# Threshold search of a two-layer mixer kernel: counts spread over TensorE's work, elementwise products moved to GpSimd

## The chip, the cores and the metric

The kernel runs on one core of a Trainium2 chip. The metric is the time on the device in microseconds (us), the lower the better. Three runs of the kernel before gave 668.64, 673.66 and 677.35 us; their median is 673.66 us.

## The reference, cut to what matters

Two layers of a mixer are computed for one prompt of 256 tokens and for 8 sequences with 4 new tokens each, so 288 token columns in all, and in each layer three branches: sparse attention whose keys are chosen by an indexer (the 256 best of 2,052 positions for a sample token), dilated window attention, and a state-space scan (SSD). Everything is float32.

```python
for l in range(DEPTH):                                    # 2 layers
    hp, kv, ki, dil, conv, ssd = layer_prompt(hp, prm)
    hs, kv, ki, dil, conv, ssd = layer_sample(hs, cache_dsa_kv, cache_dsa_kidx, l, page_table, dil_bufs, ...)

# in a layer
(q_a, k_a, v_a, g_a, qi, ki, wi, q_c, k_c, v_c, g_c, z, xbc, dt) = project(rms_norm(x, norm_w), w_in)
q_a, k_a, qi, ki, q_c, k_c = rope_partial(...)            # x * cos + partner(x) * sin
sc = indexer_scores(qi, wi, ki_all)
_, idx = lax.top_k(sc, n_sel)                             # found here as a threshold
o_a = sparse_attend(q_a, k[idx], v[idx])
o_c, new_bufs = dilated_sample(q_c, k_c, v_c, bufs)       # new_bufs: the old cache, shifted by 4
seg = acs[i] - acs[j];  scores = (C B^T) * exp(seg) * dt  # SSD, 6 heads
y = y_diag + (C h_in) * exp(acs);  y = (y + d_skip * xs) * silu(z)
x = x + merge_out(o_a, g_a, o_c, g_c, y, w_out)
```

The outputs include the shifted window caches (`new_bufs`), which are copies from memory to memory.

## The kernel before, in words

**Tiling.** A layer projects the 288 columns through 35 weight tiles of 128 output rows (QI 0 to 3, KI 4, QA 5 and 6, XBC 7 to 13, KA 14 and 15, ZZ 16 to 18, QC 19 to 21, KC 22 to 24, VC 25 to 27, GC 28 to 30, VA 31 and 32, GA 33 and 34), each 8 steps of k (`proj(i)`), and through 8 tiles of the output matrix. The code is written by hand, one program for each engine, with semaphores between them; the order of each program is the order of the work, and no scheduler changes it. All matrix products go through one helper, `mm` (L825), all transposes through `turn` (L875).

**Weights.** A tile's weights are 512 KB. Four slots hold them; SyncE's queue (SP) loads tile i + 4 when tile i has been computed (`next_w`, L425).

**Cache records.** The pages of keys and values and the windows go through a ring of 8 slots. A slot is loaded again when TensorE has used it, in turn by SP and by GpSimd's queue (L404, L397).

**Cache copies.** `keep(b, use)` (L496) issues three copies from memory to memory on GpSimd's queue, 2,044, 508 and 124 KB for a sequence, once projection tile `use` has been computed: tiles 16 to 21, 23 and 24.

**The search.** The 256th best score is found bit by bit. In `compare(n)` (L1453) VectorE compares 516 scores in each of 128 rows with the trial value and sums the hits; in `bit_count(n)` TensorE adds up the row segments in one small product; in `settle(n)` (L1464, L1466) VectorE sets the bit. That is done 32 times, and each step needs the one before. Between them stand, on TensorE, the projection tiles 16 to 26 with three counts in each tile (after k steps 2, 5 and 7), the transposes of the SSD inputs, and the six SSD heads (`head(h)`), which end with the row of decays for the head after the next (`bc`). On VectorE stand, after a compare and ahead of its settle, the rotary products (`rope`, L1408 to L1413: a shuffle and three products of 128x288), the inputs of the state sums (`state_inputs`, L1716), the heads' exponents and factors (`lin`, `g_mul`) and the gated outputs (`y_out`, L1755 and L1759). GpSimd has `masked` (L518: the state inputs of one sequence) and the spreading of the dilated queries (L539, L543).

**After it.** With the threshold known, a mask is built (L1943), spread by TensorE, added to the scores (L1949), and the exponentials (L766) are transposed; then come the value records, the other projections and the output product.

Of the kernel before, what the change touches and what calls it, by code (L numbers as in the profile page):

```python
# [18 lines left out]
ALU = mybir.AluOpType  # L19
# [3 lines left out]
P = 128  # L23
# [3 lines left out]
TP = 256  # L27
# [107 lines left out]
def bank_plan():  # L135
# [33 lines left out]
    for name, bank in (("ad", 7), ("xs0", 5), ("bt0", 3), ("bt1", 2), ("xs2", 6), ("xs1", 7), ("bt2", 3), ("knt", 6), ("cb", 2),  # L169
                       ("lastj", 6), ("cbs", 6), ("st0", 5), ("st1", 3)):  # L170
        use(name, bank)
# [25 lines left out]
    "rstd_ready": 1, "sq_ready": 8, "sq_used": 7, "y_normed": 8, "xw_ready": 8, "xn_free": 7, "xn_ready": 8, "roped": 15, "ssum_ready": 1, "root_ready": 1,  # L197
# [4 lines left out]
    "dec_ready": 1, "xws_ready": 1, "ea_ready": 6, "lin": 6, "lexp": 6, "g_ready": 6, "yh_used": 3, "dn_used": 1,  # L202
# [7 lines left out]
def build(nc, a):  # L210

    plan, _ = bank_plan()
    with ExitStack() as ctx:
        def sb(name, shape, dt=F32):
# [16 lines left out]
        tmp = sb("tmp", [P, T])  # L231
        misc = sb("misc", [64, T])
# [76 lines left out]
             for name in ("x_in0", "x_in1", "ptab_in", "prm_in", "cst_in", "const_in", "ones_set", "zeroed", "act_chain", "dve_chain", "y_out",  # L309
# [69 lines left out]
        def w_count(layer, i):  # L379

            return 16 * ((layer * NW + i) // WSLOTS + 1)

# [100 lines left out]
        def _(pool):  # L483
            POOL = mybir.EngineType.Pool
            pool.wait_ge(S["ptab_in"], 16)
# [3 lines left out]
            for L in range(DEPTH):  # L489
# [30 lines left out]

                keep(0, "proj16")
# [3 lines left out]
                keep(1, "proj17")  # L525
                keep(2, "proj18")
                pool.wait_ge(S["xws_ready"], nth(L, "xws_ready", 1))
# [12 lines left out]
                for g in range(3):  # L540
                    for h2 in range(2):
                        q = ptile(QC + g, TP, T, half(h2)).rearrange("p (b q) -> p b q", q=NQ)
                        pool.tensor_copy(qcbd[half(h2), g, :, h2:2 * NB:2], q.rearrange("p b q -> p q b")).then_inc(S["qcbd_ready"], 1)  # L543
                keep(6, "proj23")
                keep(7, "proj24")
                consumed(*RING[32:40])
# [25 lines left out]
        def _(act):  # L572
# [20 lines left out]
            for L in range(DEPTH):  # L593
# [137 lines left out]
                evac(18)  # L731
                act.wait_ge(S["adt_ready"], nth(L, "adt_ready", 1))
                act.activation(dec[:, 0:2, :], dec[:, 0:2, :], ACT.Exp).then_inc(chain.next(), 1)
                act.activation(dec[0:32, 2, :], dec[0:32, 2, :], ACT.Exp).then_inc(S["dec_ready"], 1)
                evac(19)
                act.wait_ge(filled("cbs"), nth(L, "cbs"))
                act.activation(cbs[:, :], bank_of("cbs")[0:32, 0:64], ACT.Copy).then_inc(drained("cbs"), 1)
                act.wait_ge(filled("st0"), nth(L, "st0"))
# [3 lines left out]
                evac(20)  # L742

                def ssd_exp(h):
# [3 lines left out]
                    if h >= 2:  # L748
                        act.wait_ge(S["g_ready"], nth(L, "g_ready", h - 1))

                    act.wait_ge(S["lin"], nth(L, "lin", h + 1))
                    act.activation(ea[:, h % 2, :], src[:, 0:T], ACT.Exp).then_inc(S["ea_ready"], 1)
# [3 lines left out]
                    act.activation(lg[0:32, h % 2, TP:T], lg[0:32, h % 2, TP:T], ACT.Exp, bias=nacs[0:32, 2, h:h + 1]).then_inc(S["lexp"], 1)  # L756

# [63 lines left out]
        def _(pe):  # L821
# [16 lines left out]
            for L in range(DEPTH):  # L838
# [13 lines left out]
                def proj(i, *counts):  # L852


                    at = {len(counts): (3, 7)[:len(counts)], 3: (2, 5, 7)}[len(counts)]

                    wt = weights(i)
                    pe.wait_ge(drained(f"proj{i}"), before(L, f"proj{i}"))
                    out = bank_of(f"proj{i}")
                    for k in range(KT):  # L860
# [4 lines left out]
                        ins = mm(out[:, 0:T], wt[:, k, :], xn[:, k, :], start=(k == 0), stop=(k == KT - 1))  # L865
                        if i == LATE_ROOT - 1 and k < KT - 1:
                            ins.then_inc(S["xn_free"], 1)
                        if k in at and k < KT - 1:
                            bit_count(counts[at.index(k)])
                    ins.then_inc(filled(f"proj{i}"), 1)  # L870
                    if KT - 1 in at:
                        bit_count(counts[-1])
# [242 lines left out]
                proj(16, 0, 1, 2)  # L1115
# [6 lines left out]
                ins.then_inc(filled("ad"), 1)  # L1122
                pe.wait_ge(S["conved"], nth(L, "conved", 7))
# [5 lines left out]
                proj(17, 3, 4, 5)  # L1129
                token_rows("xs", 1, XBC, 3)  # L1130
                token_rows("bt", 2, XBC + 3, 2)
                pe.wait_ge(S["roped"], nth(L, "roped", 9))
# [6 lines left out]
                pe.wait_ge(drained("cb"), before(L, "cb"))  # L1139
                out = bank_of("cb")  # L1140
                for g in range(2):
                    for c in range(2):
                        ins = mm(out[:, g * 256 + c * P:g * 256 + (c + 1) * P], ptile(XBC + 3 + g, c * P, (c + 1) * P),
                                 ptile(XBC + 5 + g, c * P, (c + 1) * P))
                ins.then_inc(filled("cb"), 1)

                proj(18, 6, 7, 8)
                pe.wait_ge(drained("ad"), nth(L, "ad"))
# [1043 lines left out]
```

## Time and profile before

| | us |
|---|---|
| median of 3 runs | 673.66 (668.64 to 677.35) |
| the profiled execution, its own time | 673.8 |
| its span, first to last instruction | 672.1 |
| TensorE busy (matmul) | 611.9 (91%) |
| VectorE, GpSimd, ScalarE busy | 377.8, 224.0, 168.1 |
| chain that ended last: TensorE, VectorE, DMA | 63%, 15%, 13% |
| mean granted TensorE clock | 0.962 |
| moved by DMA | 198.38 MB, 295 GB/s in the mean |

The search of the first layer lies at 113 to 202 us of the span, that of the second at 435 to 525 us. A granted clock of 1.0 is 2.4 GHz, 0.5 is 1.2 GHz. An instruction that waits shows its wait as idle time ahead of it, with what ended it.

### The profile page before, as it was taken

Reading aid. Unit: us, or ns where it says so; the run is one execution under the profiler, and the core shown is the slowest. Engines: PE = TensorE matmul, PEld = TensorE weight load, DVE = VectorE, ACT = ScalarE, POOL = GpSimd, SP = SyncE. Lnnn points to the kernel's source line nnn. Section 1 sums busy time; section 2 is a strip of 40 time slices with the busy share of each in tenths; the row PEclk is TensorE's granted clock in tenths of the full one; section 3 lists DMA queues with packets and bytes.
Section 4 is the critical chain, followed back from the end, with each engine's and each line's share of the span. In section 5 each row is a group of like instructions: output and inputs, shape, how many; then the busy total and the mean of one; then the engine's idle time right before and its main releaser. Section 6 shows DMA issues by size and latency. Waiting matters only on the chain.

```text
span 672.1 us, 13786 instructions
## 1 busy us (share of the span) xinstructions
PE 611.9 (91%) x4870; PEld 426.9 (64%) x4870; DVE 377.8 (56%) x1150; ACT 168.1 (25%) x405; POOL 224.0 (33%) x406
## 2 busy tenths in 40 slices
PE   5999998888899989999999999988888989789994
PEld 3766564665567665667776656566665867556772
DVE  3765565677569545443167475577756855343413
ACT  3024222121113312451101433212201151126211
POOL 0507530241206676451000664124120377642000
PEclk9999999898889998999999999999878999889998
DMA  7979999999968989996334999999997598996031
GB/s 294 308 274 356 368 369 413 417 358 331 353 236 262 314 305 369 366 329 234 110 121 134 323 368 369 402 413 355 349 394 265 181 333 287 374 357 214 10 118 70
DMA packets 67766, 198.38 MB, mean 295 GB/s; under 512 B 11537, under 2 KB 40370, under 8 KB 66418
## 3 DMA queue, kind: packets, MB, share of 16 engines
q1 hardware_dynamic: 49682, 99.99, 42.8%
q0 software_dynamic: 18016, 97.50, 40.3%
q8 instruction: 39, 0.64, 0.4%
q14 instruction: 29, 0.24, 0.1%
HBM read 189.30 MB, written 52.00 MB: 359 GB/s over the span
## 4 chain that ended last, share of the span: by engine, by line
PE 63%; DVE 15%; DMA 13%; ACT 4%; issue 2%; SPq 2%; DVEq 0%; ACTq 0%
PE bank L825 60%; DMA w<-in_w 5%; DMA kv<-in_vv 4%; DMA kv<-in_kk 4%; DVE hit L1453 3%; PE bank L875 3%; SPq L404 2%; DVE tb L1466 1%; DVE st L1955 1%; ACT srow L766 1%; ACT shared L663 1%; DVE tb L1464 1%; DMA x<-in_x 1%; DVE shared L1576 1%; ACT shared L680 1%
## 5 line engine op out<-in xcount | busy, mean ns | idle before, releaser
L825 PE MATMUL bank<-xn,w 128*128 128x288 f32 x1120 | 307.0, 429 | 0.7 <-DMA w<-in_w 0.7
L825 PEld LDWEIGHTS bank<-xn,w 128*128 128x128 f32 x1120 | 213.9, 198 | 74.9 <-issue 19.1
L404 POOL DMA_DIRECT2D kv<-in_vv x160 | 86.3, 539 | 96.9 <-PE bank L825 69.5
L404 POOL DMA_DIRECT2D kv<-in_kk x128 | 68.8, 538 | 144.5 <-issue 96.1
L616 ACT ACTIVATE pt<-bank 128x288 f32<-128x288 f32 x48 | 19.6, 409 | 243.4 <-PE bank L825 243.4
L825 PE MATMUL bank<-pt,w 128*128 128x288 f32 x256 | 64.9, 407 | 0.0
L825 PEld LDWEIGHTS bank<-pt,w 128*128 128x128 f32 x256 | 48.3, 190 | 13.6 <-issue 0.8
L496 POOL DMA_DIRECT2D out_keep<-in_buf x48 | 23.5, 495 | 85.1 <-PE bank L825 78.7
L1453 DVE TENSOR_SCALAR_CACHE_REDUCE hit<-sc,tb 128x516 bf16<-128x516 f32 x62 | 46.5, 750 | 2.2
L825 PE MATMUL bank<-kv,pt 128*32 128x256 f32 x512 | 37.5, 404 | 11.0 <-DMA kv<-in_vv 10.7
L1464 DVE TENSOR_SCALAR tb<-bank 128x1 int32<-128x1 f32 x62 | 9.5, 153 | 48.7 <-PE bank L825 48.5
L825 PE MATMUL bank<-kv,qz 128*32 128x256 f32 x512 | 34.3, 385 | 0.0
L2022 DVE TENSOR_TENSOR x<-x,bank 128x288 f32<-128x288 f32 x16 | 7.3, 455 | 43.6 <-PE bank L825 43.3
L825 PEld LDWEIGHTS bank<-cnt,seg 128*128 128x128 f16 x68 | 6.9, 103 | 38.8 <-issue 36.7
L825 PE MATMUL bank<-cnt,seg 128*128 128x1 f16 x68 | 11.2, 169 | 21.8 <-DVE hit L1453 21.1
L1426 DVE COPY tails<-cin 128x3 f32<-128x3 f32 x14 | 7.2, 512 | 41.0 <-ACT cin L614 38.9
L825 PEld LDWEIGHTS bank<-kv,pt 128*32 128x32 f32 x512 | 14.1, 112 | 22.5 <-DMA kv<-in_vv 9.5
L825 PE MATMUL bank<-kv,shared 128*32 128x128 f32 x768 | 26.8, 285 | 0.0
L825 PE MATMUL bank<-pt 64*128 64x128 f32 (+3 forms) x168 | 26.3, 334 | 0.0
L518 POOL TENSOR_SCALAR xwb<-xws,const 32x384 f32<-32x384 f32 x16 | 21.2, 1329 | 13.4 <-DVE xws L1716 7.7
L583 ACT ACTIVATE phased<-x 128x288 f32<-128x288 f32 x24 | 10.5, 442 | 60.0 <-DVE x L2022 57.1
L825 PEld LDWEIGHTS bank<-pt 64*128 64x128 f32 (+2 forms) x168 | 17.9, 183 | 10.6 <-issue 9.8
(238 smaller groups left out, 796.7 us busy)
## 6 DMA issues: line engine op xcount, KB each, us to landing
w<-in_w SPq DMA_DIRECT2D x86, 512.0 KB, 7.3
out_keep<-in_buf POOLq DMA_DIRECT2D x16, 2044.0 KB, 13.0
kv<-in_kk SPq DMA_DIRECT2D x128, 160.0 KB, 8.2
kv<-in_kk POOLq DMA_DIRECT2D x128, 160.0 KB, 5.8
kv<-in_vv POOLq DMA_DIRECT2D x160, 128.0 KB, 5.6
kv<-in_dil SPq DMA_DIRECT2D x24, 576.0 KB, 7.5
kv<-in_vv SPq DMA_DIRECT2D x96, 128.0 KB, 7.3
out_keep<-in_buf POOLq DMA_DIRECT2D x16, 508.0 KB, 8.5
```

Source lines behind the costliest of these rows:

```text
L404: engine.dma_start(kv[:, s, r * rec:(r + 1) * rec], a["kk" if what == "page" else "vv"][bass.ds(page + layer * N_POOL, 1)].rearrange("o p ...
L496: pool.dma_start(a[f"keep{g}"][ly, b], a[f"buf{g}"][ly, b, 4 * 256:]).then_inc(S["copied"], 16)
L518: pool.tensor_scalar(xwb[:, b % 2, :], xws[0:32, 2, :], C("bm", b, b + 1, slice(0, 32)), None, ALU.mult).then_inc(S["xwb_ready"], 1)
L583: act.activation(squares[:, k % 2, 0:T], x[:, k, :], ACT.Square).then_inc(S["sq_ready"], 1)
L616: act.activation(ptile(i), src[:, 0:T], fn).then_inc(use, 1)
L663: act.activation(psa[:, i, 0:nk], psa[:, i, 0:nk], ACT.Exp, bias=st8[:, 1, i:i + 1], accum_out=st8[:, 2, i:i + 1]).then_inc(S["pexp"] if i ...
L825: return pe.matmul(out, lhsT, rhs, start=start, stop=stop, skip_group_check=True, **k)
L875: return pe.transpose(out, in_, ident(n))
L1426: dve.tensor_copy(tails[:, n, 0:3], cin[:, n % 2, TP:TP + 3]).then_inc(chain.next(), 1)
L1453: ts_(hit[:, :], sc[:, :], old.bitcast(F32), 0.0, ALU.is_ge, ALU.add, accum_out=cnt[:, 0:1]).then_inc(S["cnt_ready"], 1)
L1464: ts_(tb[:, 2:3], src[:, 0:1], float(TOPK_S), float(bit), ALU.is_lt, ALU.mult).then_inc(drained(f"count{n}"), 1)
L2022: tt_(x[:, m, :], x[:, m, :], src[:, 0:T], ALU.add).then_inc(drained(f"out{m}"), 1)
```

## The change

Counts may now stand at any k step of a tile: `proj(i, lo, hi)` computes a part of a tile, and the counts are written between parts of tiles, groups of transposes and halves of heads. Five kinds of work go from VectorE to other engines. The three products of seven ropes (n = 8 to 14), the state inputs and the gating of y go to GpSimd; the shuffle stays on VectorE and gets a second buffer, `rstd`. The two small copies to `ebc` go to ScalarE. Three memsets that only signalled are gone. The cache copies keep their conditions, but GpSimd's program has other work ahead of and between them. The mask products move from between window products 5 and 6 into tile 27, after its second k step; tile 20 now comes before the `knt` products and the state sums, and `cb` and `lastj` before tile 18.

```diff
@@ GpSimd
+                def rope(n):
+                    i, s = ROPED[n], partner[n % 2][:, :]
+                    pool.wait_ge(S["shuffled"], nth(L, "shuffled", n - 7))
+                    pool.tensor_tensor(s, s, C("sin"), ALU.mult).then_inc(chain.next(), 1)
+                    pool.tensor_tensor(ptile(i), ptile(i), C("cos"), ALU.mult).then_inc(chain.next(), 1)
+                    pool.wait_ge(S["pool_chain"], chain.n)
+                    pool.tensor_tensor(ptile(i), ptile(i), s, ALU.add).then_inc(S["roped"], 1)
...
+                rope(8)
                 keep(0, "proj16")
...
                 keep(1, "proj17")
+                state_inputs()
                 keep(2, "proj18")
...
                 keep(3, "proj19")
+                rope(9)
                 keep(4, "proj20")
+                rope(10)
                 keep(5, "proj21")
+                rope(11)
...
+                rope(12)
                 keep(6, "proj23")
+                y_gated(0)
+                rope(13)
                 keep(7, "proj24")
+                rope(14)
+                y_gated(1)
+                y_gated(2)
                 consumed(*RING[32:40])
@@ TensorE
-                proj(16, 0, 1, 2)
+                proj(16, 0, 5)
+                bit_count(0)
+                proj(16, 5)
...
+                for h in range(1, 5):
+                    if h < 4:
+                        bit_count(13 + 3 * h)
+                    else:
+                        bit_count(25)
+                    proj(21 + h, 0, 5)
+                    bit_count(14 + 3 * h)
+                    proj(21 + h, 5)
+                    head(h, 15 + 3 * h)
+                proj(26, 0, 2)
+                bit_count(28)
+                proj(26, 2, 6)
+                bit_count(29)
+                proj(26, 6)
+                head(5, 30)
                 window_keys(0)
-                window_keys(1)
+                bit_count(31)
@@ VectorE
                 compare(17)
-                rope(10)
+                lin(2)
                 settle(17)
-
                 compare(18)
+                shuffle(12)
                 settle(18)
...
-                y_out(2)
...
-                rope(14)
```

TensorE's program, first at tile 22 and head 1 (`xn,w` are k steps of the tile, `cnt,seg` is a count, `cacc,xw`, `cs,xws` and `cs,phased` are the head, `ad,const` is `bc`). Before:

```order
L825 MATMUL bank<-xn,w 128x288 x3
L825 MATMUL bank<-cnt,seg 128x1
L825 MATMUL bank<-xn,w 128x288 x3
L825 MATMUL bank<-cnt,seg 128x1
L825 MATMUL bank<-xn,w 128x288 x2
L825 MATMUL bank<-cnt,seg 128x1
L825 MATMUL bank<-cacc,xw 64x128 x2
L825 MATMUL bank<-cacc,xw 64x32
L825 MATMUL bank<-cs,xws 64x128
L825 MATMUL bank<-cs,phased 64x4 x8
L825 MATMUL bank<-ad,const 128x288
```

The same place now:

```order
L872 MATMUL bank<-xn,w 128x288 x5
L872 MATMUL bank<-cnt,seg 128x1
L872 MATMUL bank<-xn,w 128x288 x3
L872 MATMUL bank<-cacc,xw 64x128 x2
L872 MATMUL bank<-cacc,xw 64x32
L872 MATMUL bank<-cs,xws 64x128
L872 MATMUL bank<-cnt,seg 128x1
L872 MATMUL bank<-cs,phased 64x4 x8
L872 MATMUL bank<-ad,const 128x288
L872 MATMUL bank<-cnt,seg 128x1
```

There are three counts for a tile and a head in both, but the gaps between them, in k steps, were 3, 2 and 3 with a head inside the last; now they are 5, 3 with the first part of the head, and the head's second part with `bc`.

VectorE's program around compare 20 (`hit` is the compare, the two `tb` rows are the settle). Before:

```order
L1453 TENSOR_SCALAR hit,cnt<-sc,tb 128x516
L1408 STREAM_SHUFFLE tmp<-pt 128x288
L1410 TENSOR_TENSOR tmp<-tmp,const 128x288
L1411 TENSOR_TENSOR pt<-pt,const 128x288
L1413 TENSOR_TENSOR pt<-pt,tmp 128x288
L1464 TENSOR_SCALAR tb<-bank 128x1
L1466 TENSOR_SCALAR tb<-tb 128x1
```

And now, around compares 21 and 22:

```order
L1550 TENSOR_SCALAR hit,cnt<-sc,tb 128x516
L1517 STREAM_SHUFFLE rstd<-pt 128x288
L1561 TENSOR_SCALAR tb<-bank 128x1
L1563 TENSOR_SCALAR tb<-tb 128x1
L1550 TENSOR_SCALAR hit,cnt<-sc,tb 128x516
L1827 TENSOR_TENSOR cs<-ea,pt 128x160
L1829 TENSOR_TENSOR cacc<-cacc,bank 128x256
L1830 TENSOR_TENSOR cacc<-cacc,cbs 32x32
```

Of a rope only the shuffle is left between a compare and its settle, and a head's factors no longer share a slot with the next head's exponents.

GpSimd's program from the copies behind tile 21 on. Before:

```order
L496 DMA out_keep<-in_buf 16x1984
L496 DMA out_keep<-in_buf 16x8128
L496 DMA out_keep<-in_buf 32x16352
L539 COPY shared<-pt 64x32 x6
L543 COPY qcbd<-pt 64x4x8 x6
```

And now:

```order
L502 DMA out_keep<-in_buf 16x1984
L502 DMA out_keep<-in_buf 16x8128
L502 DMA out_keep<-in_buf 32x16352
L531 TENSOR_TENSOR rstd<-rstd,const 128x288
L532 TENSOR_TENSOR pt<-pt,const 128x288
L534 TENSOR_TENSOR pt<-pt,rstd 128x288
L575 COPY shared<-pt 64x32 x6
L579 COPY qcbd<-pt 64x4x8 x6
L531 TENSOR_TENSOR tmp<-tmp,const 128x288
L532 TENSOR_TENSOR pt<-pt,const 128x288
L534 TENSOR_TENSOR pt<-pt,tmp 128x288
```

Two ropes now stand between these copies and those behind tile 23, each of which waits for a shuffle.

## Rows read from the trace of the kernel before

**Rows 1.** The page: DMA throughput in 40 equal slices of the span.

```profile
GB/s 294 308 274 356 368 369 413 417 358 331 353 236 262 314 305 369 366 329 234 110 121 134 323 368 369 402 413 355 349 394 265 181 333 287 374 357 214 10 118 70
```

**Rows 2.** Waits of TensorE: waiter, releaser, us in total, times, longest.

```profile
PE bank L825 <- DVE hit L1453: 21.1, 20, 1.7
PE bank L825 <- DMA kv<-in_vv: 10.7, 8, 2.6
PE bank L825 <- DMA w<-in_w: 0.7, 1, 0.7
```

**Rows 3.** Timeline of TensorE, tile 22 to 23 of layer 2: start, us, work.

```profile
474.96 0.16 PE L825 MATMUL bank<-cnt,seg 128*128 128x1 f16 x1 [1.20 <-DVE hit L1453]
475.19 0.85 PE L825 MATMUL bank<-cacc,xw 128*64 128x128 f32 x6
...
476.24 1.04 PE L825 MATMUL bank<-cs,phased 128*64 128x4 f32 x16
477.21 0.81 PE L825 MATMUL bank<-ad,const 6*128 6x288 f32 x2
477.95 3.25 PE L825 MATMUL bank<-xn,w 128*128 128x288 f32 x6
...
485.14 0.16 PE L825 MATMUL bank<-cnt,seg 128*128 128x1 f16 x1 [1.23 <-DVE hit L1453]
...
532.62 4.15 PE L825 MATMUL bank<-xn,w 128*128 128x288 f32 x16
```

**Rows 4.** Windows, the heads' stage of each layer: busy, clock, DMA share, GB/s.

```profile
155.00:203.00 48.00, 42.92 (x240) 30.55 (x239) 31.18 (x121) 6.35 (x21) 5.90 (x18) 0.86 0.84 304
480.00:527.00 47.00, 41.07 (x237) 28.89 (x239) 30.10 (x115) 6.75 (x23) 5.89 (x18) 0.84 0.85 304
```

**Rows 5.** Timeline of VectorE, a search step with nothing else in it.

```profile
146.47 0.75 DVE L1453 TENSOR_SCALAR_CACHE_REDUCE hit<-sc,tb 128x516 bf16<-128x516 f32 x1
...
147.58 0.16 DVE L1464 TENSOR_SCALAR tb<-bank 128x1 int32<-128x1 f32 x1 [0.35 <-PE bank L825]
...
148.02 0.75 DVE L1453 TENSOR_SCALAR_CACHE_REDUCE hit<-sc,tb 128x516 bf16<-128x516 f32 x1
```

**Rows 6.** Groups by line, VectorE at 112 to 209 us: a rope product.

```profile
L1410 DVE TENSOR_TENSOR tmp<-tmp,const 128x288 f32<-128x288 f32 x7 | 3.2, 458 | 0.2
```

**Rows 7.** DMA queues at 140 to 170 us: packets, MB, share.

```profile
q0 software_dynamic: 383, 9.45, 88.4%
q1 hardware_dynamic: 358, 1.30, 13.6%
```

**Rows 8.** The chain that ended last, at 460 to 500 us.

```profile
467.85 30.89 DMA w<-in_w
```

**Rows 9.** Loads of weights at 160 to 170 us, and of all 11 at 112 to 205 us.

```profile
w<-in_w SPq DMA_DIRECT2D x1, 512.0 KB, 23.5
...
DMA to landing us min/median/max: 3.4/14.5/25.6
```

**Rows 10.** Timeline of TensorE: tile 22's end, the window products of each layer, the transposes.

```profile
161.94 1.22 PE L825 MATMUL bank<-xn,w 128*128 128x288 f32 x4
...
203.29 1.52 PE L825 MATMUL bank<-kv,shared 128*32 128x128 f32 x48
...
216.33 1.09 PE L875 MATMUL bank<-const,srow 128*128 128x128 f32 x8 [0.70 <-ACT srow L766]
...
526.50 1.52 PE L825 MATMUL bank<-kv,shared 128*32 128x128 f32 x48
```

**Rows 11.** Groups by line, GpSimd, both layers.

```profile
L518 POOL TENSOR_SCALAR xwb<-xws,const 32x384 f32<-32x384 f32 x16 | 21.2, 1329 | 13.4 <-DVE xws L1716 7.7
L543 POOL COPY qcbd<-pt 64x32 f32<-64x32 f32 x12 | 3.2, 263 | 0.7
```

**Rows 12.** The chain that ended last, first layer, around the mask.

```profile
209.56 1.88 DVE srow L1949 x3
...
214.18 2.10 ACT srow L766 x2
```

More of the change, by code:

```diff
@@ L850, in weights, with proj @@
                     return w[:, slot, :, :]
[L852 to L860, printed above, removed]
+                def proj(i, lo=0, hi=KT):
+                    wt = w[:, (L * NW + i) % WSLOTS, :, :]
+                    if lo == 0:
+                        weights(i)
+                        pe.wait_ge(drained(f"proj{i}"), before(L, f"proj{i}"))
+                    for k in range(lo, hi):
                         if i == 0:
@@ L1127, in _ @@
                 token_rows("xs", 2, XBC, 3)
-                proj(17, 3, 4, 5)
+                proj(17, 0, 1)
+                bit_count(2)
+                proj(17, 1, 6)
+                bit_count(3)
+                proj(17, 6)
                 token_rows("xs", 1, XBC, 3)
                 token_rows("bt", 2, XBC + 3, 2)
+                bit_count(4)
+                pe.wait_ge(drained("cb"), before(L, "cb"))
+                out = bank_of("cb")
+                for g in range(2):
+                    for c in range(2):
+                        ins = mm(out[:, g * 256 + c * P:g * 256 + (c + 1) * P], ptile(XBC + 3 + g, c * P, (c + 1) * P),
+                                 ptile(XBC + 5 + g, c * P, (c + 1) * P))
+                ins.then_inc(filled("cb"), 1)
+                pe.wait_ge(drained("ad"), nth(L, "ad"))
+                pe.wait_ge(drained("lastj"), before(L, "lastj"))
+                out = bank_of("lastj")
+                for c in range(2):
+                    mm(out[:, 6 * c:6 * c + 6], C("lastp"), adt[:, c, 0:6])
+                mm(out[0:32, 12:18], C("last", rows=slice(0, 32)), adt[0:32, 2, 0:6]).then_inc(filled("lastj"), 1)
+                bit_count(5)
+                proj(18, 0, 4)
+                bit_count(6)
+                proj(18, 4)
+                bit_count(7)
+                proj(19, 0, 4)
+                bit_count(8)
+                proj(19, 4)
+                bit_count(9)
+                pe.wait_ge(drained("cbs"), before(L, "cbs"))
+                out = bank_of("cbs")
+                for g in range(2):
+                    ins = mm(out[0:32, g * 32:g * 32 + 32], ptile(XBC + 3 + g, TP, T), ptile(XBC + 5 + g, TP, T))
+                ins.then_inc(filled("cbs"), 1)
+                proj(20, 0, 3)
+                bit_count(10)
+                proj(20, 3, 7)
+                bit_count(11)
+                proj(20, 7)
                 pe.wait_ge(S["roped"], nth(L, "roped", 9))
```

210 lines of the change are left out of this document (104 added, 106 removed).

## The prediction

> **What bounds the kernel now.** I read four things in this order: what TensorE waits for, its timeline in the search, the granted clock there, and what the DMA queues carry meanwhile.
>
> TensorE is busy for 91% of the span, and in the table of its waits one line stands out: 21.1 us in 20 waits for the compare of the search; weights cost it 0.7 us, value records 10.7 us [rows 2]. The timeline of a tile and a head shows where [rows 3]. The third count comes two k steps after the second, 1.2 us of work [rows 10], but a bare search step takes 1.55 us from one compare to the next [rows 5], and before this count VectorE had more to do. So TensorE stands 1.2 us, does the head, whose second half is 16 tiny products, and `bc`, and then the first six matmuls of the next tile take 3.25 us, where a whole tile of 16 takes 4.15 us elsewhere [rows 3]. Six should take 1.55 us: 1.7 us are lost to the clock, which is 0.86 and 0.84 in the mean of the two heads' stages [rows 4] and so falls from 2.4 to 1.2 GHz in each of these stretches. The clock did not fall behind the last two heads of the first layer, where the stall was 1.06 us and no `bc` followed, or where it was 0.24 us. One period is 10.18 us (474.96 to 485.14) [rows 3].
>
> The third party is DMA. It is 84% busy in these stages [rows 4], and from 101 to 185 us it moves 331 to 417 GB/s [rows 1]. At 140 to 170 us the queue of the cache copies (q0) moves 9.45 MB and that of the weights (q1) 1.30 MB, with nearly the same number of packets, 383 and 358 [rows 7]. The engines take them in turn, and a copy's packet is seven times as large, so weights come in at 43 GB/s, 12 us for a tile of 512 KB, as long as copies are queued. A load then takes 23.5 us [rows 9], and once 30.9 us: the load of tile 24 of the second layer starts when tile 20 ends, at 467.85, and lands when tile 24 wants to start [rows 8]; that is the 0.7 us of wait [rows 2].
>
> **The change part by part.**
>
> *Counts between parts of tiles.* The 32 steps of a layer were 1.2 to 1.7 us apart where VectorE needs 1.55 us plus its extra work. I set the new gaps on TensorE against VectorE's need. A k step is 0.5 us, so the gaps in the heads' stage are 5 k steps (2.6 us), 3 k steps and the head's first part (1.55 + 1.05), and the second part with `bc` (1.0 + 0.75). VectorE's longest extra work there is a head's factors (about 0.9 us, of which 0.35 us hide in the count's own latency [rows 5]), 2.1 us in all. Only two early gaps (ahead of counts 2 and 13) come out short, by 0.1 and 0.3 us. So the stall of 10.6 us per layer goes, 21.1 us in all, less about 1 us.
>
> *The clock.* With no stall ahead of a head the 1.7 us behind it should go too: four times in the first layer, five in the second, 15.3 us, and 1.7 us once early in the first layer.
>
> *Work moved from VectorE.* Seven ropes lose three products of 0.46 us each per layer [rows 6], y gating three, the state inputs three. All lay beside TensorE's work or are in the stalls counted above, so I add nothing. The copies to `ebc` on ScalarE: nothing, it is 25% busy and a head has 7 us.
>
> *GpSimd.* It takes 21 rope products, 3 state products and 3 gating products per layer. None is in the trace. From below, a product costs VectorE's 0.46 us [rows 6]; from above, twice the 1.33 us that GpSimd takes for a one-input product of 384 columns [rows 11], cut to 288, is 2.0 us. I take 1.3 us, nearer the row of the same engine, so a rope is 4 us. Every tile period gives it one rope, 1.5 us of issuing copies, and once 3.6 us of spreading: it keeps up. Copies leave up to 2 us late, which costs nothing while the copies before them are still queued. The Trainium skill (GPSIMD Engine Reference, "Performance versus the Vector engine") measures a two-input product of 2,048 columns at 4,497 ns against 2,293 ns; by that one of 288 columns would be near 0.9 us, an estimate, and the sum would be the same.
>
> *GpSimd beside VectorE.* In the 3.6 us in which GpSimd spreads queries, VectorE's product takes 0.46 us as ever, so I take 0. If VectorE's work were stretched by a fifth, the gaps above would still cover it.
>
> *The mask.* VectorE goes from mask to scores without `rope(14)`, but TensorE now has only 6 k steps of tile 27 (3.1 us) and 2.3 us of small products between the mask product and the transposes, while additions, maximum and exponential take 6.7 us (209.56 to 216.28) [rows 12] and start 0.25 us after. TensorE waits some 1.4 us where it waited 0.7 [rows 10]: +0.7 us per layer.
>
> *The weights.* All of this moves TensorE's wish for tiles 20 to 26 forward, and the copies' too, but not the bytes. By the parts above, a period in the heads' stage is a tile of 4.1 us, a head of 2.0 and a `bc` of 0.75: 6.9 us instead of 10.2. The weights' queue, however, is never empty: loads are asked for every 5 to 10 us, when a tile ends, and land 14.5 us later in the median [rows 9]. So an earlier request lands no earlier. In the first layer the load of tile 26 starts when tile 22 ends (161.94 + 1.22) and lands 23.5 us later [rows 9, 10], at 186.8 us; tile 26 and the last head take 6.1 us, so the window products start at 192.9 us where they started at 203.3 [rows 10]: a gain of 10.4 us. In the second layer tile 24 cannot start before 498.8 [rows 8]; it and its head take 6.9 us, tile 25 6.2 (no `bc`), tile 26 6.1: 518.0 instead of 526.5 [rows 10], a gain of 8.5 us. The tiles between land within these bounds. Without the weights the same points would come at 182 and 504 us.
>
> **The sum.** 10.4 + 8.5 = 18.9 us, less 1.4 us for the two masks, less 1.7 us for one slow stretch behind the long wait that tile 24 of the second layer then has (8 us): 15.8 us. The profiled execution took 673.8 us, 0.1 us from the median of three, so 658 us. The Trainium skill (DMA: Bandwidth & Descriptors, "Queues, rings and completion order") says that each DMA engine goes round its queues by packets, and the equal packet counts agree with it; it speaks for the weights keeping their small share. If they had half of the bytes instead, a load would land in 3 to 4 us and the sum would be the second rival's.
>
> **The rivals.**
>
> *Same pace* (chance 0.22). Weights land up to 2 or 3 us later than I assume, since the copies are asked for earlier too; each wait at a tile's start stands beside a weak head, so the slow clock stays for several tiles, and the last of them is not hidden. For it: the weights' rate of 12 us a tile is above the old period of 10.2 us, and loads in the second layer are later than in the first. Then 2 to 10 us are gained: 664 to 672, say 667.
>
> *Weights keep up* (chance 0.17). A deeper queue or copies that leave later let loads land with the requests. Stalls and clock give 21.4 and 22.1 us, less 1.4: 632 us. But the copies still need their time: 10 us of their traffic in each layer would then run into the value records, for which TensorE waits already [rows 2]. With that 640 to 650, say 645.
>
> *GpSimd sets the pace* (chance 0.06, the slower side). Its program is one queue: products, then copies, then the loads of value records. From the copies of tile 19 to the first value load it has 70 us now, less 11 us of copies and spreading, for 21 products: 2.8 us each. Above that value loads and window queries come later than before; at 3.5 us it is 15 us per layer, 700 us with the gain gone. Against it: both bounds above lie below 2.8 us. It decides only from there.
>
> *The clock stays low* though stalls go, because the heads' tiny products are enough: that is inside the first rival and my own range, since waiting for weights hides it.
>
> My forecast has 0.55. Its own range is 650 to 665.
>
> **The numbers.** 658 us; the range of 642 to 671 leaves out the best part of the second rival, the third, and the end of the first. The runs before spread by 9 us, so 2% (13.5 us) is about what can be told from no change. Faster by over 2% means under 660.2: six tenths of my forecast and all of the second rival with a part of the first, 0.54. Within 2%: 0.39. Slower: 0.07.
>
> **What would show it.** The waits for compares under 3 us instead of 21.1. New waits of TensorE for `in_w`, 10 to 25 us in all, at the starts of tiles 22 to 26, with loads that take over 25 us. The packets of the two queues near one to one while copies run. GpSimd's product of 288 columns at 0.7 to 2.0 us, and its value loads no later after the last head than before. Granted clock in the heads' stage over 0.86. Window products 10 and 8 us earlier against the start of the search. I am wrong if TensorE waits neither for weights nor for compares (then it is the second rival), or if the wait for weights is there and the ends do not move (the first).

## The result and the profile after

The change makes the kernel slower by 1.8%: 685.55 us (682.46 to 689.48, 4 runs) against 674.07 us (668.64 to 677.35, 4 runs), a ratio of 1.018 with a 95% interval of 1.013 to 1.024. It is slower beyond the noise, but whether by more than 2% is not settled. The forecast was 658 us with a range of 642 to 671. The profiled execution took 684.6 us; its span is 682.9 us, 10.8 us over that of the kernel before. In all that follows a median is that of all runs of a kernel, and a ratio leaves out runs that took over 1.5% more than the quickest.

TensorE's waits in the changed kernel (columns as in [rows 2]):

```profile
PE bank L872 <- DMA w<-in_w: 17.6, 7, 3.6
PE bank L872 <- DMA kv<-in_vv: 8.1, 7, 2.6
PE bank L917 <- ACT srow L813: 4.4, 2, 2.2
PE bank L872 <- DMA kv<-in_kk: 3.6, 5, 1.4
PE bank L872 <- ACT xws L787: 2.0, 2, 1.0
```

The wait for the compare, 21.1 us in [rows 2], is gone from the table. Waits for weights have taken its place, 17.6 us where there were 0.7. Two waits for ScalarE are larger or new: for the exponentials (2.2 us in each layer) and for the copies of the state sums (1.0 us).

TensorE's timeline in the first layer shows where (start, us, work, the wait ahead in brackets):

```profile
169.37 4.38 PE L872 MATMUL bank<-xn,w 128*128 128x288 f32 x10 [1.20 <-DMA w<-in_w]
181.98 5.17 PE L872 MATMUL bank<-xn,w 128*128 128x288 f32 x10 [3.57 <-DMA w<-in_w]
194.60 2.29 PE L872 MATMUL bank<-xn,w 128*128 128x288 f32 x4 [3.58 <-DMA w<-in_w]
204.19 0.86 PE L872 MATMUL bank<-kv,shared 128*32 128x128 f32 x24
204.99 0.18 PE L872 MATMUL bank<-cnt,seg 128*128 128x1 f16 x1
...
219.05 3.83 PE L917 MATMUL bank<-const,srow 128*128 128x128 f32 x16 [2.21 <-ACT srow L813]
```

Tiles 24, 25 and 26 each wait for weights, and ten matmuls behind such a wait take 4.4 to 5.2 us, where ten take 2.7 us elsewhere (a row of e1 below). The window products start at 204.19; they started at 203.29 [rows 10]. The transposes, which started at 216.33 [rows 10], start 2.7 us later, and the 16 of them take 3.83 us.

The chain that ended last, around the end of each search, now runs through the load of tile 26:

```profile
157.91 36.64 DMA w<-in_w
...
486.92 39.06 DMA w<-in_w
```

The load lands at 194.55 in the first layer, 36.64 us after it was asked for; [rows 8] had 30.89 us at the worst. The queues at 140 to 170 us:

```profile
q0 software_dynamic: 384, 9.49, 89.5%
q1 hardware_dynamic: 381, 1.36, 13.6%
...
w<-in_w SPq DMA_DIRECT2D x3, 512.0 KB, 31.8
```

As many packets on one queue as on the other, those of the copies seven times as large in the mean, 45 GB/s for the weights: the picture of [rows 7], with a median landing time of 31.8 us. (What these counts hold is looked at under e10.) The heads' stages, as in [rows 4]:

```profile
155.00:203.00 48.00, 39.65 (x199) 27.34 (x197) 25.31 (x83) 7.16 (x29) 14.30 (x29) 0.82 0.86 300
480.00:527.00 47.00, 37.72 (x205) 26.69 (x204) 24.66 (x85) 8.08 (x35) 18.15 (x35) 0.83 0.98 342
```

The granted clock (the third number from the end) did not rise from 0.86 and 0.84; it fell to 0.82 and 0.83.

**Where the 10.8 us lie.** Four points of TensorE's timeline cut the span: the first window product of each layer (the search has ended), and the single transpose ahead of the output product. I use the same cuts for the experiments.

| kernel (span) | search 1 ends | to output 1 | to end of search 2 | to output 2 | rest |
|---|---|---|---|---|---|
| before (672.1) | 203.3 | 102.9 | 220.3 | 106.0 | 39.6 |
| after (682.9) | 204.2 | 110.4 | 220.9 | 107.8 | 39.7 |
| e1 after, no copies (648.1) | 188.6 | 109.0 | 202.3 | 108.6 | 39.6 |
| e2 before, no copies (671.0) | 204.5 | 106.2 | 215.5 | 105.2 | 39.6 |
| e5 two copies behind the search (674.4) | 192.0 | 116.4 | 208.1 | 118.1 | 39.7 |
| e8 tile 28 earlier (672.4) | 203.3 | 105.3 | 218.6 | 105.6 | 39.7 |
| e10 copies in smaller rows (694.5) | 188.7 | 133.0 | 204.3 | 128.8 | 39.7 |
| e13 copies asked for later (670.0) | 198.1 | 109.7 | 210.6 | 111.9 | 39.6 |
| e15 best (650.5) | 187.9 | 102.6 | 208.3 | 106.5 | 45.2 |

So the searches gained nothing (+0.9 and +0.6 us), and 9.3 us were lost between the searches and the output products. A row is one execution: that of e8 is the quickest of its six (674.1 us, where the median is 679.6), that of e13 the slowest of its four (671.7, where the median is 667.2).

The experiments ran in groups, each beside the kernel before, whose median was 671.6 to 676.2 us. Ratios are to that of the same group; a difference in us between kernels of two groups can be off by some 5 us.

### The profile page after: what moved, and what is told of

Its sections match the earlier page's. It is cut to its first block, busy times and chain, and to the rows that moved or that the text cites. A ratio compares the mean times of both kernels' runs of the same rounds, so it can differ in the third digit from the quotient of the medians.

```text
span 682.9 us, 13776 instructions
## 1 busy us (share of the span) xinstructions
PE 623.0 (91%) x4870; PEld 435.0 (64%) x4870; DVE 359.0 (53%) x1058; ACT 175.8 (26%) x433; POOL 267.1 (39%) x460
## 4 chain that ended last, share of the span: by engine, by line
PE 64%; DMA 21%; DVE 6%; ACT 4%; SPq 2%; issue 2%; ACTq 0%; DVEq 0%; POOLq 0%; POOL 0%
PE bank L872 61%; DMA w<-in_w 11%; DMA kv<-in_kk 6%; DMA kv<-in_vv 3%; PE bank L917 3%; SPq L409 2%; DVE shared L1673 1%; DVE st L2032 1%; ACT srow L813 1%; ACT shared L707 1%; DVE xw L1860 1%; ACT shared L724 1%; DVE st L1679 1%; DVE srow L2026 1%; DMA x<-in_x 1%
## 5 line engine op out<-in xcount | busy, mean ns | idle before, releaser
L872 PE MATMUL bank<-xn,w 128*128 128x288 f32 x1120 | 311.2, 435 | 17.6 <-DMA w<-in_w 17.6
L872 PEld LDWEIGHTS bank<-xn,w 128*128 128x128 f32 x1120 | 218.5, 201 | 93.4 <-DMA w<-in_w 18.2
L872 PE MATMUL bank<-kv,pt 128*32 128x256 f32 x512 | 39.6, 422 | 10.7 <-DMA kv<-in_vv 8.1
L872 PEld LDWEIGHTS bank<-kv,shared 128*32 128x32 f32 x768 | 22.9, 118 | 4.3 <-issue 2.3
L872 PEld LDWEIGHTS bank<-pt 64*128 64x128 f32 (+2 forms) x168 | 17.9, 183 | 11.0 <-issue 10.2
L550 POOL TENSOR_TENSOR pt<-pt 128x288 f32<-128x288 f32 x6 | 4.8, 798 | 48.8 <-DVE pt L1836 48.8
```

The source lines that it names most:

```text
L872: return pe.matmul(out, lhsT, rhs, start=start, stop=stop, skip_group_check=True, **k)
```

## The experiments

**Theory.** Weights and copies share the DMA engines by packets. At the new pace tiles ask for weights every 7.3 us, and the copies, which wait for tiles, are asked for earlier as well. They go ahead of the weights of the last tiles, so the search ends when it ended before. Rivals: GpSimd's new work costs the time; the new order itself is worse; what is taken from one stage only reappears in the next.

**e1 and e2, without the copies.** What does the order give when nothing competes with the weights?

```diff
-                    for g in range(3):
-                        pool.dma_start(a[f"keep{g}"][ly, b], a[f"buf{g}"][ly, b, 4 * 256:]).then_inc(S["copied"], 16)
...
-            pool.wait_ge(S["copied"], DEPTH * PER["copied"])
```

> The changed kernel with the window cache copies left out (its output lacks them). Packet turns (the copies' large packets starve the weights' queue): TensorE's waits for weights in the heads' stage fall from 17.6 us in all to under 2, the clock there rises above 0.95, the window products of the first layer start 18 to 22 us earlier than 204.2, and the kernel takes 630 to 645 us. GpSimd or the new order itself is what costs: the search ends where it did, within 5 us of 204.2, and the kernel stays above 665 us.

> The kernel before with the window cache copies left out (its output lacks them). It is the partner of the kernel above. Packet turns: its search waits for compares, not for weights, so the 21 us of stalls and the slow clock stay and only the waits for value records shrink: 660 to 670 us, so the new order is worth 20 to 30 us without copies. If the new order is what costs, this one is the faster of the two.

Measured: 651.51 us (ratio to before 0.971, 0.964 to 0.978) and 672.12 us (0.998, 0.995 to 1.002). The changed order alone is worth 20.6 us. The copies cost the kernel before nothing and cost the changed one 34 us, 15.6 and 18.6 us of it in the two searches (the table). Both runs are 2 to 7 us above what was expected, and the window products of e1 start 15.6 us earlier, not 18 to 22. Waits of TensorE in e1:

```profile
PE bank L869 <- DMA kv<-in_vv: 11.8, 9, 3.7
```

No line for weights is left in its table. The expected 630 to 645 us was too low by 6: one reason is in its timeline, at the start of tile 23 of the first layer:

```profile
157.66 1.09 PE L869 MATMUL bank<-cs,phased 128*64 128x4 f32 x16
158.68 0.75 PE L869 MATMUL bank<-ad,const 6*128 6x288 f32 x2
159.36 0.18 PE L869 MATMUL bank<-cnt,seg 128*128 128x1 f16 x1
159.40 4.31 PE L869 MATMUL bank<-xn,w 128*128 128x288 f32 x10
...
168.28 2.67 PE L869 MATMUL bank<-xn,w 128*128 128x288 f32 x10
```

TensorE stands nowhere here, and still the ten matmuls at 159.40 run at half clock; those at 168.28 do not.

**e3 and e4, copies in rows of 4 KB**, written in alternating order so that rows are not joined again.

```diff
-                        pool.dma_start(a[f"keep{g}"][ly, b], a[f"buf{g}"][ly, b, 4 * 256:]).then_inc(S["copied"], 16)
+                        n = (992, 1016, 1022)[g]
+                        dst, src_ = (v.rearrange("o (r two n) -> (o two) r n", two=2, n=n)
+                                     for v in (a[f"keep{g}"][ly, b], a[f"buf{g}"][ly, b, 4 * 256:]))
+                        pool.dma_start(dst, src_).then_inc(S["copied"], 16)
```

> The changed kernel with the same copies in rows of 4 KB in alternating order, so that a packet of a copy is no larger than one of the weights. Packet turns: the weights' queue gets near half of the bytes, the waits for weights in the search fall from 17.6 us to under 4, window products of the first layer start 12 to 20 us earlier, the copies end later and run into the value records; 645 to 660 us. Total bandwidth is the bound: loads of weights land no earlier, or the whole traffic is slower with small packets, and the kernel takes 680 us or more.

> The kernel before with the copies in rows of 4 KB. Packet turns: it waits 0.7 us for weights, so it has nothing to win and the copies may reach further into the value records: 668 to 680 us. Total bandwidth, with small packets less efficient: above 680 us, and the same loss would lie in the changed kernel.

Measured: 934.09 and 933.24 us, ratio 1.391 for both. A load of weights in the search of e3 landed in 8.3 us in the median, against 22.8 in the changed kernel. The times fall under the second expectation of each, 680 us and more, but in form only: I did not expect a loss of 260 us. In the trace the copies' packets have 8,176 bytes, the size of two rows, so they are still twice the 4 KB of the weights'. And something larger happened. GpSimd's timeline in e3:

```profile
131.12 1.43 POOL L505 DMA_DIRECT2D out_keep<-in_buf  x2
173.38 1.60 POOL L505 DMA_DIRECT2D out_keep<-in_buf  x1 [40.82 <-issue]
```

Between two parts of one copy GpSimd stands 40.8 us with nothing that it waits for; I read it as a full queue, which no row names. Everything behind it in its program comes late, ropes and value loads. So this pair says little about shares.

**e10, rows of 16 KB**, the milder form of the same question: `n = (992, 4064, 4088)[g]`.

> The changed kernel with copies in rows of 16 KB for the two large parts, same places, same bytes. Shares go by packets: the weights' queue gets a larger share of the bytes beside copies, a load in the search lands in under 25 us where it took 31.8, waits for weights fall below 10 us while the copies end later, 676 to 684 us. Shares do not depend on the size of packets: landing times and waits as before, 684 to 688 us. GpSimd held up in issuing, as with rows of 4 KB: waits for compares come back, above 700 us.

Measured: 697.11 us (1.035, 1.030 to 1.041). The time is outside all three expectations, but the parts are the clearest of the study. The queues at 150 to 190 us in e10:

```profile
q0 software_dynamic: 3456, 11.23, 74.1%
q1 hardware_dynamic: 712, 2.61, 17.5%
```

The same stretch of the changed kernel:

```profile
q0 software_dynamic: 477, 12.18, 87.0%
q1 hardware_dynamic: 477, 1.76, 13.3%
```

Beside shorter rows the weights get 2.61 instead of 1.76 MB of nearly the same total. A load in the search lands in 12.5 us in the median instead of 22.8, TensorE waits for no weights at all, and the first search ends at 188.68 us, as without copies (188.55). The copies pay: they land in 33.2 us instead of 18.2 and reach far into the next stage, where TensorE then waits for value records:

```profile
PE bank L875 <- DMA kv<-in_vv: 46.8, 13, 15.4
```

The weights were starved by their share, and that share depends on the length of the copies' rows. How the engines take turns these runs do not settle. By the rows above the packets stand 4.9 to 1 in e10 and one to one in the changed kernel, but many of them carry next to nothing. All packets of e10 in that stretch, and those of the changed kernel:

```profile
DMA packets 4170, 13.87 MB, mean 347 GB/s; under 512 B 2821, under 2 KB 2821, under 8 KB 3499
...
DMA packets 956, 13.97 MB, mean 349 GB/s; under 512 B 249, under 2 KB 249, under 8 KB 743
```

Those under 512 bytes are of 4 and 8 bytes. Without them the copies' queue has 710 packets to 637 of the weights' in e10, nearly one to one, and 276 to 429 in the changed kernel, where they are of 64, 32 and 8 KB against 4 KB.

**e5, two copies behind the search.** The copies of sequences 6 and 7 leave behind tile 26.

```diff
-                keep(6, "proj23")
...
-                keep(7, "proj24")
...
                 feat(KC, KC + 3, 5)
+                keep(6, "proj26")
+                keep(7, "proj26")
                 masked(2)
```

> The changed kernel with the last two copies of each layer (sequences 6 and 7, asked for at tiles 23 and 24) moved behind tile 26 and the key columns' output. Demand above supply: while tiles take 7 us, eight copies and the weights want more than the engines move, and the weights are the side that waits; without two copies the waits for weights in the search fall from 17.6 to under 5 us and the first window products start 10 to 14 us earlier, but the two copies then run beside the value records: 664 to 678 us. New order or GpSimd at fault: 683 us or more.

Measured: 678.07 us (1.008, 1.004 to 1.011), at the upper edge of the expectation; the waits for weights are 6.4 us, not under 5. Waits:

```profile
PE bank L872 <- DMA kv<-in_vv: 17.2, 11, 3.6
...
PE bank L872 <- DMA w<-in_w: 6.4, 2, 3.4
```

The searches end 12.2 and 12.8 us sooner, the stages behind them take 6.0 and 10.4 us longer: two thirds of the gain is given back there. The waits for value records have grown by 9.1 us (17.2 against 8.1), which is a good half of the 16.4.

**e6, the same two copies in the output product**, `keep(6, "out0")` and `keep(7, "out4")` at the end of GpSimd's layer.

> The changed kernel with the same two copies of each layer moved to the output product (behind its tiles 0 and 4), where DMA is at half load. Demand above supply: the search as in the kernel above, the value records no later than without copies, the output tiles perhaps 2 to 5 us slower: 654 to 666 us. New order or GpSimd at fault: 683 us or more.

Measured: a median of 673.69 us in ten runs that spread from 661.4 to 677.7, the widest of all. It is above the expectation, but 12 us below the changed kernel.

**e7, the seven ropes back on VectorE.**

```diff
-                shuffle(12)
+                rope(12)
```

(the same for 8 to 11, 13 and 14, and the seven `rope` calls gone from GpSimd's program)

> The changed kernel with the three products of the seven ropes back on VectorE, everything else as changed. GpSimd's products are innocent (they take 0.8 us and copies never leave late): the time stays within 1% of 685 us, a little more if VectorE now makes TensorE wait. GpSimd's products are the cost, by delayed issues or by slowing VectorE: 670 to 677 us.

Measured: 684.99 us (1.016, 1.009 to 1.024), the changed kernel's 685.55. The rope products on GpSimd are innocent (its state inputs and gating stayed there). The waits of TensorE say more:

```profile
PE bank L865 <- DMA w<-in_w: 9.9, 4, 4.2
PE bank L865 <- DVE hit L1543: 7.6, 12, 0.7
```

7.6 us of waits for compares came back, and the waits for weights shrank from 17.6 to 9.9 us. Together they are 17.5 us, and the window products start at 204.29 us where they started at 204.19: whoever makes TensorE wait, the search ends when the weights have come.

**e8, tile 28 ahead of the transposes.** It fills the wait for the exponentials.

```diff
                 state_sum(1)
+                proj(28)
                 pe.wait_ge(S["sexp"], nth(L, "sexp", 1))
...
                 value_groups(0, 4)
-                proj(28)
```

> The changed kernel with projection tile 28 ahead of the transposes of the exponentials instead of behind the first value products. Late mask: the two waits of 2.2 us for the exponentials and the half clock behind them (16 transposes in 3.8 us) go, 679 to 682 us. The value records set the time of that stage: no gain, 684 to 687 us.

Measured: 679.59 us (1.010, 1.003 to 1.017). The transposes:

```profile
219.84 1.04 PE L917 MATMUL bank<-const,srow 128*128 128x128 f32 x8
221.19 1.14 PE L917 MATMUL bank<-const,srow 128*128 128x128 f32 x8 [0.31 <-ACT pt L820]
```

The wait of 2.21 us is gone and the half clock with it: the two halves take 1.04 and 1.14 us, the 16 took 3.83. From search to output it gains 5.1 and 2.2 us. For the whole kernel the gain is not clear of noise by this run alone (the intervals, 1.003 to 1.017 and 1.013 to 1.024, overlap); e9 and e14 below bear it out.

**e9, e11, e12, combinations.** e9 is e6 with e8; e11 moves three copies, behind output tiles 0, 3 and 6; e12 is e9 with the first decay rows two k steps later, to fill the wait of 1.0 us for ScalarE:

```diff
+                proj(21, 0, 2)
+                bit_count(13)
                 bc(0)
-                bit_count(13)
                 bc(1)
-                proj(21, 0, 3)
+                proj(21, 2, 5)
                 bit_count(14)
-                proj(21, 3)
+                proj(21, 5)
```

> The changed kernel with two copies of each layer in the output product and tile 28 ahead of the transposes, both edits of the two runs before together. The two losses are separate (the copies' bytes in the search, and the late mask): the gains add, 12 and 6 us, and it takes 665 to 670 us. They are one loss (value records arrive at the same time whatever comes before): 672 us or more.

> Three copies of each layer (sequences 5, 6 and 7) in the output product, behind its tiles 0, 3 and 6, and tile 28 ahead of the transposes. Demand above supply in the search: no wait for weights is left there (under 2 us), but three copies in 50 us of output product may cost 3 to 6 us there; 658 to 668 us. If a third copy only moves the wait to the output tiles: as with two copies, 665 to 672 us.

> As the kernel with two copies moved and tile 28 earlier, and the first two decay rows behind two k steps of tile 21, so that TensorE need not wait 1.0 us for ScalarE's copy of the state sums. Stall and half clock behind it (6 steps in 3.25 us, 10 in 4.17) go: 3 to 6 us less than the kernel without this edit. The weights set the search's end anyway: the same time within 1 us.

Measured: 665.15 us (0.988, 0.982 to 0.994), 672.46 us (0.999, 0.994 to 1.003) and 663.43 us (0.986, 0.980 to 0.992). e9 did as expected. e11 missed: with the third copy 12.9 us of waits for weights lie in the output products of both layers, the longest in the first, and 4.6 us are still in the searches, where under 2 were expected:

```profile
319.16 6.76 PE L872 MATMUL bank<-pt,w 128*128 128x288 f32 x16 [5.12 <-DMA w<-in_w]
```

In e12 the wait for ScalarE is gone, but it is only 1.7 us below e9 and within the spread of both, between its two expectations (3 to 6 us less, or the same within 1), which leaves that edit open.

**e13, the copies asked for about when they were before.** The step of the forecast that failed is tested: TensorE keeps the new order, only the copies wait for later tiles (18, 19, 20, 21, 22, 24 and 25 instead of 17 to 21, 23 and 24).

```diff
-                keep(1, "proj17")
                 state_inputs()
-                keep(2, "proj18")
+                keep(1, "proj18")
...
-                keep(3, "proj19")
+                keep(2, "proj19")
                 rope(9)
-                keep(4, "proj20")
+                keep(3, "proj20")
                 rope(10)
-                keep(5, "proj21")
+                keep(4, "proj21")
...
+                keep(5, "proj22")
                 rope(12)
-                keep(6, "proj23")
                 y_gated(0)
                 rope(13)
-                keep(7, "proj24")
+                keep(6, "proj24")
                 rope(14)
                 y_gated(1)
+                keep(7, "proj25")
```

> The changed kernel with the copies asked for about when the kernel before asked for them: behind tiles 16, 18, 19, 20, 21, 22, 24 and 25. Copies overtook the weights because they were asked for earlier: the weights of tile 26 land by 187 to 190 us, the first window products start at 193 to 197 us (204.2 without the edit), waits for weights fall below 10 us, and since the end of the copies now lies beside the value records, 672 to 680 us. Only the demand of the stage counts, not the order of requests: waits for weights stay at 14 to 18 us and the time at 683 to 687 us.

Measured: 667.18 us (0.986, 0.981 to 0.991), 18 us below the changed kernel and 5 below the 672 to 680 expected. The start of tile 26:

```profile
189.24 2.29 PE L872 MATMUL bank<-xn,w 128*128 128x288 f32 x4 [7.78 <-DMA w<-in_w]
```

Its weights land at 189.2 us, as expected; in the changed kernel it was 194.55. The last two copies leave 4.4 and 3.8 us later than in the changed kernel, which is about half of the way back to the kernel before. Before, changed, and e13:

```profile
173.57 1.47 POOL L496 DMA_DIRECT2D out_keep<-in_buf  x3 [3.85 <-PE bank L825]
183.72 1.45 POOL L496 DMA_DIRECT2D out_keep<-in_buf  x3 [8.68 <-PE bank L825]
...
165.37 1.53 POOL L502 DMA_DIRECT2D out_keep<-in_buf  x3 [3.94 <-PE bank L872]
175.62 1.52 POOL L502 DMA_DIRECT2D out_keep<-in_buf  x3 [5.54 <-PE bank L872]
...
169.81 1.52 POOL L502 DMA_DIRECT2D out_keep<-in_buf  x3 [4.03 <-PE bank L872]
179.45 1.52 POOL L502 DMA_DIRECT2D out_keep<-in_buf  x3 [3.23 <-PE bank L872]
```

The queues at 117.5 to 176.5 us in e13:

```profile
q0 software_dynamic: 785, 16.88, 79.3%
q1 hardware_dynamic: 1009, 4.42, 21.0%
```

And in the changed kernel:

```profile
q0 software_dynamic: 843, 17.52, 82.3%
q1 hardware_dynamic: 914, 3.97, 18.7%
```

The copies moved 0.64 MB less in that stretch and the weights' queue 0.45 MB more, nearly a tile, at nearly the same total. The window products start at 198.1 us, 1 us later than expected, and waits for weights are still 12.0 us, above the 10 expected and below the 14 to 18 of the rival. But they are three waits (0.59, 7.78 and 3.63 us) where there were seven, each with one stretch of half clock behind it, as the seven had. So e13 shows that asking for the copies later brings the gain; how much of it is the order of the requests and how much the fewer bytes of copies in the stretch, it does not part.

**e14 and e15.** e14 is e13 with the edits of e8 and e12; e15 is e14 with the last two copies behind output tiles 0 and 4.

> As the kernel above, with tile 28 ahead of the transposes and the decay rows behind two k steps of tile 21. If these edits keep their 6 to 8 us beside it: 665 to 673 us. If the value records decide: as the kernel above, within 2 us.

> Two copies in the output product, the other six held behind tiles 16, 18, 19, 20, 21 and 22, tile 28 and the decay rows as above. The waits for weights left in the search (about 7 us) shrink since each copy comes a tile later: 658 to 663 us. The bytes only move to the value records: 662 to 667 us.

Measured: 660.46 us (0.977, 0.973 to 0.982) and 653.56 us (0.965, 0.957 to 0.972). Both are below what was expected. e15 is 3.5% faster than the kernel before. Its waits and its granted clock at 113 to 203 us:

```profile
PE bank L872 <- DMA kv<-in_vv: 14.2, 10, 4.5
PE bank L872 <- DMA w<-in_w: 7.5, 3, 3.6
```

```profile
113.00:203.00 90.00, 89.57 (x686) 66.69 (x684) 63.70 (x215) 22.17 (x66) 46.84 (x79) 0.96 0.91 329
```

TensorE is busy 89.6 of 90 us at a clock of 0.96; in the changed kernel it was 80.5 us at 0.87. Of the waits for weights that are left, 0.2 us lie in the searches and 3.6 us in each output product; the second takes 45.2 us to the end instead of 39.6.

## Why the prediction was wrong, point by point

*Counts between parts of tiles.* Right. The compare's waits went from 21.1 us to none, and a period without a wait for weights is 7.3 us (153.55 to 160.84), against 6.9 forecast.

*Work moved, GpSimd.* Right in the effect, too high in the price. VectorE's compare took 750 ns in the mean as before, so VectorE lost nothing beside GpSimd. A product of 128x288 on GpSimd:

```profile
L532 POOL TENSOR_TENSOR pt<-pt,const 128x288 f32<-128x288 f32 x7 | 5.5, 792 | 0.0
```

0.79 us against the 1.3 taken, between the bounds of 0.46 and 2.0. My estimate from the figure in the Trainium skill (GPSIMD Engine Reference, "Performance versus the Vector engine") was near 0.9 us; the trace is a little below it. e7 shows that the rope products cost nothing.

*The weights.* **The step that failed.** "So an earlier request lands no earlier" was read as: it lands at the old time. It landed later. I let TensorE's program move forward and left the copies of [rows 7] where they had been, though they wait for the same tiles. In the first layer the last two left about 8 us earlier than before (173.6 and 183.7 us there), and were moved ahead of the weights of tiles 25 and 26, which landed at 181.9 and 194.5 us; 186.8 was the forecast for the latter (its sum, 161.94 + 1.22 + 23.5, makes 186.7). In the second layer they left 5.6 and 5.8 us earlier, measured from the first copy. In the second layer tile 24 started at 501.2 us against the bound of 498.8, and the window products at 535.4, not at 518.0. So 18.9 us of gain became a loss of 1.5. e13 brought the last two requests about half of the way back and won 6.1 and 10.2 us in the two searches, with the window products at 198.1 in the first layer, and gave 4.1 us back in the stage behind the second. The share that the weights keep I read from equal counts of packets; the reading was wrong, since the counts hold packets of 4 bytes (e10). Without those, the kernel before has 217 to 318 at 140 to 170 us. The rate of 43 GB/s was read rightly, and on it the forecast rests. The first rival named this ("Weights land up to 2 or 3 us later than I assume, since the copies are asked for earlier too") but with 3 us where it was 7.7, and gave it a gain.

*The clock.* Wrong. I charged the slow stretches to stalls ahead of heads, and took 15.3 us as given back. Each of the seven new waits for weights (0.69 to 3.62 us) had such a stretch behind it, so the clock of the stage fell to 0.82. And e1 shows one with no stall ahead.

*The mask.* The mechanism was right, the size was not. I counted only the small products ahead of the transposes. What I left out is that the last count moved. VectorE's last compare and TensorE's last count before:

```profile
199.49 0.75 DVE L1453 TENSOR_SCALAR_CACHE_REDUCE hit<-sc,tb 128x516 bf16<-128x516 f32 x1
...
200.82 0.17 PE L825 MATMUL bank<-cnt,seg 128*128 128x1 f16 x1
```

And after:

```profile
203.72 0.75 DVE L1550 TENSOR_SCALAR_CACHE_REDUCE hit<-sc,tb 128x516 bf16<-128x516 f32 x1
```

with its count at 204.99. The count stood 2.5 us ahead of the window products and now stands 0.8 us behind them. In wider gaps the 32 counts reach further into the program, and everything that hangs on the threshold starts 3.3 us later against TensorE's other work. The cost was not 0.7 us per layer: the pair without copies (e1 less e2) has 2.8 and 3.4 us from search to output, and e8, which fills the wait, gets 5.1 and 2.2 us back. The wait for value records, forecast at no change, fell in sum (10.7 to 8.1 us), so it explains none of the loss.

*GpSimd sets the pace.* Fallen, by e7 and by GpSimd's own times: no product kept a copy from leaving. In the second layer the copies behind tile 23 left 2.8 us after it, at 499.42 us, but GpSimd had stood idle for 8.99 us ahead of them, and in the kernel before they left 2.8 us behind their tile as well (494.02 to 496.82).

*The slower side.* I gave it 0.07 and one mechanism. Both mechanisms at work here were in my text with too small a price, and each was only taken off the gain, never set against no gain at all.

*What stays open.* Why the stage behind the search took 7.5 us more in the first layer and only 1.8 us in the second; why the kernel before gains 4.8 us in its second search without copies and loses 3.7 us of it at the other cuts; what held GpSimd ahead of the copies behind tile 23 in the second layer; and what makes the clock fall in unbroken work.

## What to carry to other kernels

When a change speeds up an engine whose progress releases transfers, move every one of those transfers in the forecast, and ask which of two queues gains from being early: here the bulk copies, which nobody waits for, gained what the weights lost. Tie bulk copies to the pace that the demand can bear (one tile later was worth 18 us), or put them where the queues are half idle, but spaced. And when a serial chain is spread over more work, look up where its last link lands and what then starts late.

## What the runs showed of the hardware

- Two queues with work did not share the engines by bytes. Beside copies in rows of up to 64 KB the weights' queue got 1.76 of 13.97 MB at 150 to 190 us; beside copies in rows of up to 16 KB it got 2.61 of 13.87 MB, half as much again.
- Equal counts of packets (477 to 477) are no proof of equal turns: they hold packets of 4 bytes, and without these it is 276 to 429, and 710 to 637 with the shorter rows. The Trainium skill (DMA: Bandwidth & Descriptors, "Queues, rings and completion order") says that an engine goes round its queues by packets, but the packets it means are bundles of several descriptors, which no row here counts; so these runs neither bear it out nor speak against it.
- With copies in rows of 4 KB (packets of 8 KB in the trace) all traffic together was 98 to 120 GB/s in most slices of 140 to 170 us, and GpSimd stood 40.8 us in the middle of its issuing; in long rows the copies alone moved 316 GB/s (9.49 MB in 30 us).
- A two-input product of 128x288 took 0.79 us on GpSimd beside VectorE's work, and VectorE's compare took its 750 ns as before.
- The clock fell to 1.2 GHz behind all seven waits for weights of the changed kernel (0.69 to 3.62 us), and in e1 behind a head and a decay row with no wait at all (ten matmuls in 4.31 instead of 2.67 us); behind the same head and row, 9 us later in e1, it did not fall.
